# Un-normed products for the first four tiles behind a layer norm

## The chip, the cores and the metric

One NeuronCore of a Trainium2 chip runs the whole program. The metric is the device time of one execution in microseconds (us), of which less is better.

## The reference

The program computes two blocks of a transformer on 512 tokens (528 with the 16 meta tokens of the first block) of width 1024, in float32. The first block has two layers; each is a mixer and an MLP, and each of these four ends in a layer norm over the sum with the residual:

```python
h = _layernorm(DN_ALPHA * h + mix, ln_mix_g[l], ln_mix_b[l])
f = jnp.square(jax.nn.relu(h @ mlp_w1[l])) @ mlp_w2[l]
h = _layernorm(DN_ALPHA * h + f, ln_mlp_g[l], ln_mlp_b[l])
```

The mixer of layer 0 is a recurrence with attention, that of layer 1 a retention with the input projection `od_w_in`. The second block begins with `conv_w_in_2` and ends, in both of its layers, in a mixture of 64 experts. So behind each of the four norms of the first block stands a dense layer: norm 1 (`ln_mix` 0) feeds `mlp_w1` of layer 0, norm 2 (`ln_mlp` 0) feeds `od_w_in`, norm 3 (`ln_mix` 1) feeds `mlp_w1` of layer 1, and norm 4 (`ln_mlp` 1) feeds `conv_w_in_2`. A layer norm is (x - mean) * rs * g + b, where mean and rs = 1/sqrt(var + eps) belong to a token and g and b to a feature.

## The kernel before

Activations lie transposed: a feature tile of 128 features stands on the partitions and the tokens lie along the free dimension, so `hT` holds x as eight tiles of 128x528 (of 128x512 from the third norm on, where the meta tokens are dropped). The code numbers the norms l = 0 to 3; the text calls them first to fourth.

A dense layer is the generator `dense`. It makes output tiles of 128 columns. Float32 precision comes from splitting both operands into an upper and a lower part (`HS[:, 0]` and `HS[:, 1]` for the activations, `WS` for the weights) and adding three products: upper weights and lower weights times upper x, and upper weights times lower x. A tile with K = 1024 is eight k steps of three products; with 528 tokens each product is two matmuls of 264 columns, 48 in the tile, with 512 tokens one matmul of 512 columns, 24 in the tile. At a norm the first two tiles are made as a pair, k step by k step, the lower x products two steps behind, so that x may still be arriving (`pair`). `between` is a function called in front of step 4 of the pair, `late` one called in front of the last two k steps of the last tile.

Weights come by DMA from the SP queue into the five slots of `ring`, each with the weights of two tiles. ScalarE makes the upper part of a tile's weights (`split_hi`) and VectorE the lower one (`split_lo`), into one of three `WS` buffers, which is free when the tile three back is summed. Both stand in the program by hand, one for each tile, two tiles ahead of the product. Each engine executes its instructions in program order, so a split waits for all that is written ahead of it on its engine.

The sums lie in PSUM in four units of two banks that go round (`Ring`); `units.take` waits until the tile that held the unit has been read (`emptied`). `late` for a norm is `ln_first_pe`: for feature tiles 0 to 6 GpSimd has added up x (`S`) and x squared (`Q`) with `sums_pool`, and TensorE multiplies these with a vector of 1/1024 (one-column matmuls, which give the mean of each token on the partitions) and with a matrix of it (the mean of each token in a row on every partition).

Behind the last tile, `sum_dve` adds it to `hT[:, 7]`, ScalarE squares it (`square_act`), and `ln_pe` adds tile 7 to the statistics, in the units "stat" and "mean". VectorE (`ln_dve`) makes the variance, ScalarE the square root, VectorE the diagonal matrices `diag`, and TensorE spreads the root over all partitions (unit "rs"). Then eight feature tiles go through four engines: VectorE subtracts the mean row (`less`) and multiplies by g and the root (`scaled`), both with the row read from PSUM; ScalarE adds b twice, once into the upper half `HS[:, 0]` and once into `hT`; GpSimd subtracts the two into the lower half `HS[:, 1]` (`ln_pool`). The first matmul of the next layer waits for the upper half of feature tile 0.

In the MLP ScalarE applies ReLU to a w1 tile from PSUM into `tmpA`, GpSimd squares it, and ScalarE and VectorE split it into `BR`. The names in the profile are `sb_hs` for HS, `sb_ws` for WS, `sb_hT`, `sb_tmpA` (which holds S, Q, the squares and the ReLU rows), `sb_br`, `sb_VT` (g and b), `sb_cst` (the constants) and `ps` for PSUM. The text counts the tiles of the layer behind a norm from 0: the pair is tiles 0 and 1.

## Time and profile before

| | before |
|---|---|
| median of 3 runs | 3161.15 us (3158.59 to 3164.65) |
| profiled execution, first to last instruction | 3159.2 us |
| TensorE matmul busy | 2918.6 us, 92% |
| VectorE busy | 1399.3 us, 44% |
| ScalarE busy | 920.2 us, 29% |
| GpSimd busy | 608.3 us, 19% |
| share of TensorE in the chain that ended last | 86% |

The profiled execution has no time of its own in the results beside this span; what of an execution lies outside the first and last instruction is in the times of the runs alone. The four norms end near 290, 681, 1150 and 1518 us. Engines are PE (TensorE matmul), PEld (its weight loads), DVE (VectorE), ACT (ScalarE), POOL (GpSimd) and SP (its DMA queue). A line of the program is mostly that of a helper (L101 a matmul, L118 a tensor_tensor, L126 a scalar_tensor_tensor, L108 an activation, L112 a ScalarE copy), so groups are told apart by their tiles.

### The profile page before, as it was taken

How to read it: one execution, taken by the hardware profiler on the slowest of the kernel's cores; microseconds unless marked ns; L12 is line 12 of the kernel's file. 1: busy time of each engine (PE TensorE's matmuls, PEld its weight loads, DVE VectorE, ACT ScalarE, POOL GpSimd, SP SyncE). 2: the span in 40 equal slices, each digit the busy share in tenths (PEclk: the TensorE clock that was granted, in tenths of full speed). 3: DMA queues.
4: the chain of work that ended last, by engine and by line, in shares of the span. 5: the costliest groups of instructions: out<-in, count | busy, mean ns of one | idle time of the engine just before them, and what ended most of it. 6: DMA issues, size and time to landing. Idle time of an engine off the chain costs nothing.

```text
span 3159.2 us, 42475 instructions
## 1 busy us (share of the span) xinstructions
PE 2918.6 (92%) x17571; PEld 2268.3 (72%) x17571; DVE 1399.3 (44%) x2437; ACT 920.2 (29%) x1714; POOL 608.3 (19%) x534
## 2 busy tenths in 40 slices
PE   8999999999999999999999898888699997998884
PEld 7659999998888778888787555555577775555552
DVE  5634323343444543233544453323588844533234
ACT  4543313232222333142322121111335721211112
POOL 1404101120111131021100442222000002522220
PEclk9999999999999999999998899999899998999998
DMA  4012222222222222233225899999622139999996
GB/s 141 27 54 68 94 94 85 90 90 71 71 84 76 68 71 99 88 100 101 79 81 214 348 407 409 410 409 409 249 80 77 57 119 364 405 408 410 409 409 278
DMA packets 272213, 600.31 MB, mean 190 GB/s; under 512 B 32648, under 2 KB 177603, under 8 KB 255627
## 3 DMA queue, kind: packets, MB, share of 16 engines
q1 hardware_dynamic: 247552, 569.47, 47.9%
q0 software_dynamic: 23968, 27.93, 2.7%
q8 instruction: 143, 2.34, 0.3%
q14 instruction: 60, 0.48, 0.0%
q10 hardware_dynamic: 490, 0.08, 0.0%
HBM read 607.75 MB, written 39.89 MB: 205 GB/s over the span
## 4 chain that ended last, share of the span: by engine, by line
PE 86%; DVE 5%; issue 4%; ACT 2%; DMA 2%; POOL 1%; SPq 0%; ACTq 0%; DVEq 0%; POOLq 0%
PE ps L101 80%; PE ps L104 6%; DVE sb_tmpA L118 1%; DVE sb_arena L126 1%; DMA sb_arena<-in_exp_w_dram 1%; DVE sb_arena L118 1%; DVE sb_ws L118 1%; POOL sb_arena L118 0%; DMA sb_arena<-y_rows 0%; DVE sb_tmpA L129 0%; DMA sb_arena<-x_rows,sb_smallu 0%; ACT sb_arena L112 0%; ACT sb_hs L108 0%; ACT sb_hT L108 0%; DMA sb_arena<-in_x_dram 0%
## 5 line engine op out<-in xcount | busy, mean ns | idle before, releaser
L101 PE MATMUL ps<-sb_hs,sb_ws 128*128 128x264 f32 (+1 forms) x6384 | 1106.5, 335 | 17.2 <-ACT sb_hs L108 7.5
L101 PEld LDWEIGHTS ps<-sb_hs,sb_ws 128*128 128x128 f32 x6384 | 971.0, 190 | 148.2 <-issue 16.5
L118 DVE TENSOR_TENSOR sb_ws<-sb_ring,sb_ws 128x1024 fp32r<-128x1024 f32 x279 | 370.5, 1332 | 428.0 <-ACT sb_ws L112 427.5
L112 ACT CAST sb_ws<-sb_ring 128x1024 fp32r<-128x1024 f32 x279 | 290.8, 1046 | 333.6 <-PE ps L101 318.1
L101 PE MATMUL ps<-sb_arena 128*64 128x256 f32 (+18 forms) x1652 | 347.6, 420 | 26.6 <-issue 19.8
L101 PE MATMUL ps<-sb_br,sb_ws 128*128 128x264 f32 (+1 forms) x2304 | 367.4, 321 | 0.0
L101 PEld LDWEIGHTS ps<-sb_br,sb_ws 128*128 128x128 f32 x2304 | 332.4, 188 | 34.2 <-issue 0.5
L101 PE MATMUL ps<-sb_ring,sb_arena 128*64 128x256 f32 (+2 forms) x1506 | 284.0, 450 | 25.4 <-issue 22.6
L108 ACT ACTIVATE sb_arena<-ps 64x256 f32<-64x256 f32 (+6 forms) x188 | 73.8, 403 | 756.5 <-PE ps L101 733.8
L101 PEld LDWEIGHTS ps<-sb_arena 128*64 128x64 f32 (+6 forms) x1652 | 197.9, 160 | 128.7 <-issue 69.9
L104 PEld LDWEIGHTS ps<-sb_cst,sb_arena 128*128 128x128 f32 (+2 forms) x912 | 139.4, 209 | 170.6 <-DVE sb_arena L118 82.2
L118 DVE TENSOR_TENSOR sb_arena<-sb_arena,ps 64x256 f32<-64x256 f32 x128 | 54.3, 424 | 466.2 <-ACT sb_arena L108 466.1
L2705 POOL DMA_INDIRECT y_rows<-sb_arena,sb_smallu x128 | 132.7, 1037 | 642.4 <-PE ps L104 457.3
L101 PE MATMUL ps<-sb_hx,sb_arena 128*64 128x256 f32 (+1 forms) x1240 | 209.4, 449 | 26.2 <-issue 25.5
L104 PE MATMUL ps<-sb_cst,sb_arena 128*128 128x128 f32 (+2 forms) x912 | 178.1, 325 | 51.9 <-DVE sb_arena L123 20.5
L101 PEld LDWEIGHTS ps<-sb_ring,sb_arena 128*64 128x64 f32 (+1 forms) x1506 | 153.6, 145 | 94.2 <-issue 47.3
L112 ACT COPY sb_arena<-ps 128x128 f32<-128x128 f32 (+5 forms) x335 | 137.6, 449 | 279.2 <-PE ps L101 263.1
L101 PE MATMUL ps<-sb_wx,sb_arena 128*64 128x256 f32 (+1 forms) x880 | 181.2, 442 | 15.9 <-issue 15.8
L118 POOL TENSOR_TENSOR sb_tmpA<-sb_tmpA 128x528 f32<-128x528 f32 (+1 forms) x88 | 103.2, 1173 | 461.8 <-ACT sb_tmpA L108 461.8
L101 PEld LDWEIGHTS ps<-sb_hx,sb_arena 128*64 128x64 f32 x1240 | 118.0, 147 | 80.4 <-issue 46.0
L115 DVE COPY sb_arena<-ps 64x512 f32<-64x512 f32 (+3 forms) x155 | 107.6, 695 | 144.5 <-PE ps L101 123.1
L2701 POOL DMA_INDIRECT sb_arena<-x_rows,sb_smallu x128 | 133.1, 1040 | 96.7 <-DVE sb_smallu L126 45.1
(198 smaller groups left out, 2602.7 us busy)
## 6 DMA issues: line engine op xcount, KB each, us to landing
sb_ring<-in_exp_w_dram SPq DMA_DIRECT2D x113, 1024.0 KB
sb_hx<-in_exp_w_dram SPq DMA_DIRECT2D x92, 1024.0 KB
sb_arena<-in_exp_w_dram SPq DMA_DIRECT2D x66, 1024.0 KB
sb_wx<-in_exp_w_dram SPq DMA_DIRECT2D x66, 1024.0 KB
sb_ring<-in_mlp_w_dram SPq DMA_DIRECT2D x64, 1024.0 KB
sb_hT<-in_exp_w_dram SPq DMA_DIRECT2D x47, 1024.0 KB
sb_ring<-in_od_w_in_dram SPq DMA_DIRECT2D x24, 1024.0 KB
sb_ring<-in_conv_w_in_dram SPq DMA_DIRECT2D x12, 1024.0 KB
```

The source lines that it names most:

```text
L101: return self.e.matmul(o, l, r, start=start, stop=stop, skip_group_check=True)
L104: return self.e.transpose(o, i, ident)
L108: return self.e.activation(o, i, fn, bias=bias, scale=scale)
L112: return self.e.copy(o, i)
L115: return self.e.tensor_copy(o, i)
L118: return self.e.tensor_tensor(o, a, b, op)
L126: return self.e.scalar_tensor_tensor(out=o, in0=a, scalar=s, in1=b, op0=op0, op1=op1)
L2701: return e.e.indirect_dma_start(dst, None, Xh, bass.IndirectOffsetOnAxis(ap=ig[:, b:b + 1], axis=0), bounds_check=1023, oob_is_err=False)
L2705: return e.e.indirect_dma_start(Yh, bass.IndirectOffsetOnAxis(ap=isc[:, b:b + 1], axis=0), src, None, bounds_check=2047, oob_is_err=False)
```

## The change

The first four tiles (two column blocks) of the layer behind each norm take g*x, not yet normed, as their input: its upper and lower parts are made while the last product before the norm runs (`raw_act`, `raw_dve`), in free parts of the arena (`raw_of`). Since the norm of x is (x - mean) * rs * g + b, a product W(norm x) is rs * (W(gx) - mean * Wg) + Wb. Wg and Wb come out of the same product: two columns, g and b, stand behind the T tokens of each raw tile (`raw_vectors`), and `split_raw` makes the product in two halves, of T/2 and T/2 + 2 columns, in both banks of the unit, whatever T is.

The statistics of tile 7 (`ln_stats_pe`) and the root (`ln_root_pe`) are no longer made ahead of the layer but inside its pair, in front of k steps 2 and 5 (`between` becomes a table of steps). At the third norm `ln_first_pe` moves from behind the last tile into it. ScalarE copies the mean row and the root row out of PSUM (`mean_rows`), and `less` and `scaled` read the copies. The unit "stat" is gone at three norms: it lies in free columns of "mean".

The splits of the weights of tiles 2 and 3 move: one stands in front of the norm on ScalarE and behind `diag` on VectorE, one behind the last operation of the norm on both.

Each of the four raw tiles is normed behind its product: ScalarE copies Wg and Wb (`normed_vectors_act`), VectorE makes mean * Wg - product, then times rs (`normed_dve`), and ScalarE applies -1, Wb and the function (`normed_act`), which empties the unit. The other tiles of the layer take the normed x as before, and no longer start with a pair.

```diff
+        def raw_act(e, l, m):
+            T, (g, c) = span(l)[1], LNW[l]
+            ks = raw_group(l, m)
+            if m == 0 and l in half_read:
+                e.wait_ge(*summed["part", half_read[l]])
+            e.wait_ge(*dve_emptied[LNSTAGE[l], m])
+            if ks:
+                o, v = raw_vectors(l, 0, ks)
+                e.acp(o, v).then_inc(*x_hi.mark(("raw vectors", l, ks[0])))
+            e.act(raw_of(l, 0, m)[:, 0:T], of_norm(hT[:, m, :], l), ACT.Identity, scale=vec(g + "_g", 8 * c + m)).then_inc(
+                *x_hi.mark(("raw", l, m)))
+
+        def raw_dve(e, l, m):
...
+            e.stt(raw_of(l, 1, m)[:, 0:T], of_norm(hT[:, m, :], l), vec(g + "_g", 8 * c + m),
+                  raw_of(l, 0, m)[:, 0:T].bitcast(F), ALU.mult, ALU.subtract).then_inc(*x_lo.mark(("raw", l, m)))
...
+        def normed_dve(e, l, key, at, o, T):
+
+            first = span(l)[1] - T
+            mean, rs = (x[:, first:first + T] for x in mean_rows(l))
+            e.wait_ge(*act_ln["gb", key])
+            e.wait_ge(*summed[key])
+            e.wait_ge(*act_emptied["mean", l])
+            e.stt(halves(o), halves(mean), raw_vector_of(at)[0], halves(U_[key])[:, :, 0:T // 2], ALU.mult,
+                  ALU.subtract).then_inc(*dve_ln.mark(("less", key)))
+            e.wait_ge(*dve_ln["less", key])
+            e.wait_ge(*act_emptied["rs", l])
+            e.tt(o, o, rs, ALU.mult).then_inc(*dve_ln.mark(("z", key)))
+
+        def normed_act(e, key, at, o, fn, signal, mark):
+
+            e.wait_ge(*dve_ln["z", key])
+            e.act(o, o, fn, scale=-1.0, bias=raw_vector_of(at)[1]).then_inc(*signal.mark(mark))
...
+        def ln_hooks(e, units, l):
+
+            return {2: lambda: ln_stats_pe(e, l), 5: lambda: ln_root_pe(e, units.take(e, ("rs", l)), l)}
+
         def ln_act(e, l):
             g, i = LNW[l]
+            T = span(l)[1]
+            split_hi(e)
             e.wait_ge(*dve_ln["inv", l])
             n = len(span(l)[2])
             e.act(sm[:, 75:75 + n], sm[:, 70:70 + n], ACT.Sqrt).then_inc(*act_ln.mark(("rs", l)))
+            for x, what in zip(mean_rows(l), ("mean", "rs")):
+                e.wait_ge(*normed[what, l])
+                e.wait_ge(*dve_emptied["stat", l])
+                e.acp(fit(x, T), whole(U_[what, l], T)).then_inc(*act_emptied.mark((what, l)))
             for m in range(8):
...
+            split_hi(e)
...
+            split_lo(e)
+            mean, root = mean_rows(l)
 
             def less(m):
                 x = of_norm(hT[:, m, :], l)
-                e.wait_ge(*normed["mean", l])
-                e.tt(fit(x, T), fit(x, T), whole(U_["mean", l], T), ALU.subtract).then_inc(
-                    *dve_emptied.mark(("less", l, m), *([("mean", l)] if m == 7 else [])))
+                e.wait_ge(*act_emptied["mean", l])
+                e.tt(x, x, mean, ALU.subtract).then_inc(*dve_ln.mark(("less", l, m)))
...
-                e.stt(fit(x, T), fit(x, T), vec(g + "_g", 8 * c + m), whole(U_["rs", l], T), ALU.mult,
-                      ALU.mult).then_inc(*dve_emptied.mark(("scaled", l, m), *([("rs", l)] if m == 7 else [])))
+                e.wait_ge(*dve_ln["less", l, m])
+                e.wait_ge(*act_emptied["rs", l])
+                e.stt(x, x, vec(g + "_g", 8 * c + m), root, ALU.mult, ALU.mult).then_inc(*dve_ln.mark(("scaled", l, m)))
+            split_lo(e)
...
         def mlp_pe(e, units, l):
             for hf in range(2):
                 T = span(2 * l)[1]
-                dense_all(e, ("w1", l), [(2048 * hf + 256 * i, 256) for i in range(8)], 8, ln_x(2 * l), T, units)
+                cols = [(2048 * hf + 256 * i, 256) for i in range(8)]
+                if hf == 0:
+                    dense_all(e, ("w1", l), cols[:2], 8, raw_x(2 * l), T, units, True, ln_hooks(e, units, 2 * l), raw=True)
+                    cols = cols[2:]
+                dense_all(e, ("w1", l), cols, 8, ln_x(2 * l), T, units, hf > 0)
...
-            ln_pe(e, units, 2 * l + 1)
...
             for m in range(8):
                 split_hi(e)
                 square_act(e, ("out", 0), m, 0)
+                raw_act(e, 0, m)
             ln_act(e, 0)
```

VectorE at the end of the first norm, before: the last two `scaled` (the row with x2), then for each w1 tile a weight split (`sb_ws`) and a split of the squared ReLU (`sb_br`).

```order
L126 SCALAR_TENSOR_TENSOR sb_hT<-sb_hT,sb_VT,ps 128x528 x2
L118 TENSOR_TENSOR sb_ws<-sb_ring,sb_ws 128x1024
L118 TENSOR_TENSOR sb_br<-sb_tmpA,sb_br 128x528
L118 TENSOR_TENSOR sb_ws<-sb_ring,sb_ws 128x1024
L118 TENSOR_TENSOR sb_br<-sb_tmpA,sb_br 128x528
```

VectorE at the same place, with the change. The first split of weights is that of tile 3, the second that of tile 4.

```order
L126 SCALAR_TENSOR_TENSOR sb_hT<-sb_hT,sb_VT,sb_tmpA 128x528 x2
L118 TENSOR_TENSOR sb_ws<-sb_ring,sb_ws 128x1024
L126 SCALAR_TENSOR_TENSOR sb_tmpA<-sb_tmpA,sb_small,ps 128x528
L118 TENSOR_TENSOR sb_tmpA<-sb_tmpA 128x528
L126 SCALAR_TENSOR_TENSOR sb_tmpA<-sb_tmpA,sb_small,ps 128x528
L118 TENSOR_TENSOR sb_tmpA<-sb_tmpA 128x528
L118 TENSOR_TENSOR sb_br<-sb_tmpA,sb_br 128x528 x2
L118 TENSOR_TENSOR sb_ws<-sb_ring,sb_ws 128x1024
```

The second operand of `scaled` is now a row of `sb_tmpA`, no longer `ps`. In front of the splits of tiles 0 and 1 into `sb_br` stand two new operations for each tile, and the weight split of tile 4 stands behind all of them; before, the split behind the last `scaled` was that of tile 2.

ScalarE at the same place, as a piece of the difference: the last two rows of the norm, then the ReLU of the w1 tiles.

```order
 L108 ACTIVATE sb_hT<-sb_hT,sb_VT 128x528
 L112 CAST sb_ws<-sb_ring 128x1024
-L108 ACTIVATE sb_tmpA<-ps 128x528
-L112 CAST sb_br<-sb_tmpA 128x528
-L112 CAST sb_ws<-sb_ring 128x1024
-L108 ACTIVATE sb_tmpA<-ps 128x528
-L112 CAST sb_br<-sb_tmpA 128x528
-L112 CAST sb_ws<-sb_ring 128x1024
```

With the change the row of weights there is the upper part for tile 3, and what follows it is this:

```order
L112 COPY sb_small<-ps 128x2 x2
L108 ACTIVATE sb_tmpA<-sb_tmpA,sb_small 128x528
L112 CAST sb_br<-sb_tmpA 128x528
L108 ACTIVATE sb_tmpA<-sb_tmpA,sb_small 128x528
L112 CAST sb_br<-sb_tmpA 128x528
L112 CAST sb_ws<-sb_ring 128x1024
```

The ReLU of tile 0, which empties its unit, now reads what VectorE wrote in `sb_tmpA` and stands behind the copies of Wg and Wb; the upper weights of tile 4 stand behind both ReLUs.

## Rows read from the trace of the kernel before

**Rows 1.** Busy time of each engine, two stretches of 100 us among dense tiles (windows).

```profile
400.00:500.00 100.00, 100.00 (x820) 100.00 (x819) 27.78 (x27) 19.83 (x22) 2.66 (x2) 1.00 0.28 88
...
1300.00:1400.00 100.00, 100.00 (x434) 81.06 (x433) 31.28 (x33) 31.05 (x41) 13.57 (x12) 1.00 0.28 92
```

**Rows 2.** First norm in the timeline: start, us, engine, operation, xcount, [idle before <- releaser].

```profile
277.21 2.29 PE L101 MATMUL ps<-sb_cst,sb_tmpA 128*128 128x1 f32 x20
...
280.14 1.83 PE L101 MATMUL ps<-sb_hs,sb_ws 128*128 128x264 f32 x12
...
282.01 0.70 DVE L126 SCALAR_TENSOR_TENSOR sb_hT<-sb_hT,ps 128x528 f32<-128x528 f32 x1 [4.50 <-PE ps L101]
...
286.47 2.74 PE L101 MATMUL ps<-sb_tmpA,sb_cst 128*128 128x128 f32 x12
...
289.33 0.76 DVE L126 SCALAR_TENSOR_TENSOR sb_hT<-sb_hT,sb_VT,ps 128x528 f32<-128x528 f32 x1 [0.96 <-PE ps L101]
...
291.00 21.26 PE L101 MATMUL ps<-sb_hs,sb_ws 128*128 128x264 f32 x154 [1.79 <-ACT sb_hs L108]
...
291.70 11.11 POOL L118 TENSOR_TENSOR sb_hs<-sb_hT,sb_hs 128x528 fp32r<-128x528 f32 x8 [15.28 <-ACT sb_hT L108]
...
301.32 1.03 ACT L112 CAST sb_ws<-sb_ring 128x1024 fp32r<-128x1024 f32 x1
...
304.96 0.61 ACT L108 ACTIVATE sb_tmpA<-ps 128x528 f32<-128x528 f32 x1 [2.61 <-PE ps L101]
...
308.36 1.23 DVE L118 TENSOR_TENSOR sb_ws<-sb_ring,sb_ws 128x1024 fp32r<-128x1024 f32 x1 [0.24 <-ACT sb_ws L112]
...
316.96 0.61 ACT L108 ACTIVATE sb_tmpA<-ps 128x528 f32<-128x528 f32 x1 [1.02 <-PE ps L101]
```

**Rows 3.** Windows around the first norm; the PEclk column is the granted clock.

```profile
277.00:282.00 5.00, 4.97 (x40) 4.62 (x38) 0.50 (x1) 0.00 (x0) 0.00 (x0) 1.00 0.63 204
...
287.00:291.00 4.00, 2.21 (x12) 2.13 (x11) 3.04 (x6) 0.84 (x2) 0.00 (x0) 0.50 0.00 2
...
295.00:297.00 2.00, 2.00 (x15) 2.00 (x14) 2.00 (x4) 1.93 (x4) 1.93 (x2) 0.76 0.04 8
```

**Rows 4.** Timeline at norms 2 to 4: last sum, and reading of the fourth tile.

```profile
672.40 0.70 DVE L126 SCALAR_TENSOR_TENSOR sb_hT<-sb_hT,ps 128x528 f32<-128x528 f32 x1 [4.50 <-PE ps L101]
...
707.20 0.60 ACT L112 COPY sb_arena<-ps 128x528 f32<-128x528 f32 x1 [4.82 <-PE ps L101]
...
1138.62 0.69 DVE L126 SCALAR_TENSOR_TENSOR sb_hT<-sb_hT,ps 128x512 f32<-128x512 f32 x1 [1.16 <-PE ps L101]
...
1175.39 0.60 ACT L108 ACTIVATE sb_tmpA<-ps 128x512 f32<-128x512 f32 x1 [0.51 <-PE ps L101]
...
1511.64 0.69 DVE L126 SCALAR_TENSOR_TENSOR sb_hT<-sb_hT,ps 128x512 f32<-128x512 f32 x1 [3.81 <-PE ps L101]
...
1543.99 0.69 DVE L118 TENSOR_TENSOR sb_arena<-sb_tmpA,ps 128x512 f32<-128x512 f32 x1 [1.64 <-PE ps L101]
```

**Rows 5.** Groups by form, 280 to 1600 us: xcount | busy, mean ns | idle before.

```profile
L126 DVE SCALAR_TENSOR_TENSOR sb_hT<-sb_hT,sb_VT,ps 128x528 f32<-128x528 f32 x16 | 12.0, 757 | 2.1 <-PE ps L101 2.1
...
L118 DVE TENSOR_TENSOR sb_hT<-sb_hT,ps 128x528 f32<-128x528 f32 x16 | 11.0, 697 | 0.0
...
L118 POOL TENSOR_TENSOR sb_hs<-sb_hT,sb_hs 128x528 fp32r<-128x528 f32 x16 | 21.3, 1331 | 32.3 <-ACT sb_hT L108 31.4
```

**Rows 6.** Timeline of VectorE and of GpSimd, 794 to 812 us, both with SBUF operands.

```profile
794.84 4.70 DVE L118 TENSOR_TENSOR sb_tmpA<-sb_tmpA 128x512 f32<-128x512 f32 x4
...
799.46 4.55 DVE L118 TENSOR_TENSOR sb_ws<-sb_ring,sb_ws 128x1024 fp32r<-128x1024 f32 x2
...
795.62 7.31 POOL L118 TENSOR_TENSOR sb_arena<-sb_arena,sb_tmpA 128x512 f32<-128x512 f32 x4 [33.30 <-DVE sb_tmpA L118]
```

**Rows 7.** TensorE after 18.5 us without a matmul, and a window inside that time.

```profile
2256.16 1.97 PE L104 MATMUL ps<-sb_cst,sb_arena 128*128 128x128 f32 x8 [18.52 <-DVE sb_arena L123]
...
2242.00:2256.00 14.00, 0.00 (x0) 0.00 (x0) 8.65 (x9) 5.73 (x9) 0.00 (x0) 0.50 0.88 325
```

More of the change, by code:

```diff
@@ L318, in program @@
         named = {}
+        half_read = {}
         def piece(W, p0, nr, c0, n):
@@ L430, in split_lo, with dense @@
             e.tt(lo, part_view(p), hi.bitcast(F), ALU.subtract).then_inc(*w_lo.mark(p))
-        def dense(e, stage, cols, K, rhs, T, units, pair=True, between=None, order=by_columns, late=None):
+        def dense(e, stage, cols, K, rhs, T, units, pair=True, between=None, order=by_columns, late=None,
+                  raw=False):
+            between = between or {}
+            cut = split_raw if raw else split
             def next_part():
@@ L470, in dense @@
                     for k in range(kn + 2):
-                        if k == 4 and between is not None:
-                            between()
+                        if k in between:
+                            between[k]()
                         if k < kn:
@@ L663, in even_pe @@
             units.holder = [None] * 4
-            for m in dense(e, "win", CX[:4], 8, even_x, T1, main, True, lambda: tables_pe(e, side)):
+            for m in dense(e, "win", CX[:4], 8, even_x, T1, main, True, {4: lambda: tables_pe(e, side)}):
                 for c in GATES_AT.get(m, ()):
@@ L1196, in program, with raw_of @@
         LNSTAGE = [("out", 0), ("w2", 0, 1), ("out", 1), ("w2", 1, 1)]
[L1198 to L1201 removed]
+        def raw_of(l, half, k):
+            at = {0: (2112, 10560)[half] + 530 * k,
+                  2: (2112, 4762)[half] + 530 * k if k < 5 else (10560, 12150)[half] + 530 * (k - 5)}.get(
+                l, (0, 8448)[half] + 530 * k if k < 7 else (4240, 4770)[half])
+            return place_raw[:, at:at + 530]
@@ new lines, in raw_group @@
+        def raw_group(l, m):
+            late = RAW_LATE[l]
+            return tuple(k for k in range(8) if k not in late) if m == 0 else late if late and m == late[0] else ()
+        def raw_act(e, l, m):
[9 more added lines that the diff above has]
+                *x_hi.mark(("raw", l, m)))
@@ L1210, in ln_first_pe, with ln_stats_pe @@
                 for i, (o, a) in enumerate(stat[n * c:n * c + n]):
-                    e.mm(o, part[:, a:a + 128], onesn[:, 0:1], i == 0, False)
-            for o, a, b in split(units.take(e, ("mean", l)), T):
-                e.mm(o, onesn, s[:, a:b], True, False)
-        def ln_pe(e, units, l):
-            _, T, blocks = span(l)
-            x7, q7, diag = (of_norm(x, l) for x in (hT[:, 7, :], SQ1, SQ0))
-            n = len(blocks)
-            stat = stat_of(U_["stat", l], l)
+                    e.mm(o, part[:, a:a + 128], onesn[:, 0:1], i == 0 and (c == 0 or T == T1), False)
+            for o, a, b in split(u, T):
+                e.mm(o, onesn, s[:, a:b], T == T2, False)
+        def ln_stats_pe(e, l):
+            T, n = span(l)[1], len(span(l)[2])
+            x7, q7 = (of_norm(x, l) for x in (hT[:, 7, :], SQ1))
+            stat = stat_of(l)
             e.wait_ge(*dve_emptied[LNSTAGE[l], 7])
             for o, a in stat[0:n]:
-                t = e.mm(o, x7[:, a:a + 128], onesn[:, 0:1], False, True)
-            t.then_inc(*normed.mark(("first", l)))
+                e.mm(o, x7[:, a:a + 128], onesn[:, 0:1], False, True)
+            for o, a, b in split(U_["mean", l], T):
+                e.mm(o, onesn, x7[:, a:b], False, True)
             e.wait_ge(*act_ln["sq", l, 7])
@@ L1227, in ln_pe, with ln_root_pe @@
                 t = e.mm(o, q7[:, a:a + 128], onesn[:, 0:1], False, True)
-            t.then_inc(*normed.mark(("stat", l)))
-            for o, a, b in split(U_["mean", l], T):
-                t = e.mm(o, onesn, x7[:, a:b], False, True)
             t.then_inc(*normed.mark(("mean", l)))
-            uc = units.take(e, ("rs", l))
+        def ln_root_pe(e, uc, l):
+            _, T, blocks = span(l)
+            diag = of_norm(SQ0, l)
             for i, (t0, tn) in enumerate(blocks):
@@ L1258, in ln_dve @@
             st, diag = U_["stat", l], of_norm(SQ0, l)
-            e.wait_ge(*normed["first", l])
+            q = 512 if T == T1 else n
+            e.wait_ge(*normed["mean", l])
             e.cp(mu, st[:, 0:n]).then_inc(*dve_ln.mark())
@@ L1336, in mlp_act @@
                     out_splits(e, split_hi, m)
+                    if hf and m == 6:
+                        for k in range(6):
+                            raw_act(e, 2 * l + 1, k)
                     if hf:
                         square_act(e, ("w2", l, 1), m, 2 * l + 1)
+                    if hf and m >= 6:
+                        raw_act(e, 2 * l + 1, m)
             ln_act(e, 2 * l + 1)
```

167 lines of the change are left out of this document (125 added, 42 removed).

## The prediction

> **What bounds the kernel now.** I looked first at busy time by stretches of 100 us. Where dense tiles follow each other TensorE is 100% busy at full clock: 820 matmuls of 264 columns in 100 us, so 0.122 us each and 5.87 us for a tile of 48, and 434 of 512 columns, so 5.54 to 5.56 us for a tile of 24 [rows 1]. Only TensorE can be the bound there. The change touches the four places where that stream breaks, so I read the first of them in the timeline [rows 2]. VectorE starts to add out tile 7 at 282.01, which I take as zero. The first matmul of w1 starts at 291.00, the pair of tiles 0 and 1 is read at 304.96 (+22.9) and tile 3 at 316.96 (+34.9). Four tiles at 5.87 would have ended at +23.5: **each norm costs about 11 us**. In those 11 us the reader is to see a chain (statistics, a root, `less` and `scaled` on VectorE, bias on ScalarE) and a granted clock that falls to 0.50, after 1.00 shortly before [rows 3]. The other three look alike: from the last sum to the reading of the fourth tile 34.8, 36.8 and 32.35 us [rows 4]. So at most 4 x 11 us = 44 us could be had, and less, since the statistics and the root are TensorE work that stays.
>
> **The change, part by part (first norm; times from zero).**
>
> *Product first.* Tiles 0 and 1 need only g*x, split during the out tiles. TensorE no longer waits: 96 matmuls are 11.7 us. Inside the pair lie the statistics, the same 24 instructions as in the late block of tile 7, which runs from 277.21 to 280.14, 2.9 us [rows 2]; I take 3.0. The root is 12 instructions, 2.74 us at half clock [rows 2]; bounds 1.4 and 2.7, and I take 1.5, since the stream before it is dense. The pair ends at 11.7 + 3.0 + 1.5 = 16.2 and tile 2 at 22.1. Until here the change gains 6.7 us. The two added columns of a half (2 of 264) cost 0.04 us a tile; where T is 512 each matmul of 512 becomes two of 256 and 258, at 0.119 us each (between the two paces of rows 1) 5.7 instead of 5.55 us a tile. Both are nothing beside what follows.
>
> *Raw halves.* Eight more ScalarE and eight more VectorE operations per norm, 0.7 to 0.76 us each. In an out tile of 5.87 us VectorE has a weight split of 1.2 to 2.1, a sum of 0.70 and now 0.76: covered. In the w2 stages six come at once in front of sum 6: 6 x 0.7 us on VectorE, which moves that sum back by 0.7 to 1.0 us; its squares and their sums on GpSimd still end before the late block needs them. I cost this at nothing; if the cover went it would be about 1 us at two norms.
>
> *The chain of the norm.* Statistics end at 2.0 (two k steps) + 3.0 = 5.0. The small VectorE operations, the square root and the diagonals end at 7.4, but the root stands behind k steps 2 to 4 (36 x 0.122 = 4.4), so it starts at 9.4 and ends at 10.9; its copy out of PSUM (0.6) ends at 11.5. In the kernel before, the first `scaled` starts 7.3 after zero. **The norm starts 4 us later than before**: that is the price of standing inside the product.
>
> *less and scaled.* Sixteen VectorE operations, now with both tensors in SBUF where the second was in PSUM. Before they took 0.70 and 0.76 us and went at 1.3 us a pair while GpSimd subtracted beside them in 1.33 us each [rows 2, 5]; neither slowed the other. Rows with two SBUF operands look otherwise: four VectorE operations of 512 columns took 4.70 us together and the weight splits behind them 4.55 us for two, while four of GpSimd took 7.31, where one alone is near the 1.33 above [rows 6]. Laid on one line, 4 x 0.6 + 2 x 1.07 + 4 x 1.17 = 9.2 us is what lies between 794.84 and 804.01: they take turns and nothing overlaps (0.6, 1.07 and 1.17 are estimates of the work without its start-up, from the rows above: 0.70, 1.23 and 1.33 less 0.1 to 0.15). Here GpSimd's eight subtractions follow `scaled` two ScalarE operations behind; six of them fall between the first and the last `scaled`, and each holds VectorE for 1.33 less 0.2 = 1.14 us. So the eighth `scaled` ends at 11.5 + 0.8 + 7 x 1.2 (8.4) + 6 x 1.14 (6.8) = 27.5; without turns at 20.7.
> The Trainium skill says the same in "SBUF — State Buffer", section "SBUF: two separate sides": the port pair shared by VectorE and GpSimd is an exclusive lock, taken by a VectorE operation with two SBUF inputs, and the loser blocks. By that rule the `less` of before, with one input in PSUM, was free of it and the new one is not; the trace agrees for tensor_tensor (4.70 us for four) and shows no scalar_tensor_tensor with two SBUF inputs beside GpSimd.
>
> *Tile 3.* Its weight split stands behind all of this on both engines, and its PSUM unit is that of tile 0, which must be normed and read first. After the last `scaled`: the remaining bias operations at 1.39 us a pair (the pace of the eight subtractions, 11.11 us [rows 2]) until 29.7, ScalarE's half of the weights (1.03) 30.7, VectorE's (1.23, and 0.24 of waiting for its turn) 32.2, then for tile 0 mean*Wg - product 0.7, times the root 0.7, ReLU 0.6: 34.2. **TensorE stands from 22.1 to 34.2.** Tile 3 ends at 34.2 + 5.9 = 40.1 against 34.9. Tile 4's weight split comes after both tiles' norms and their br splits, at 41.0: 0.9 us more. Sum for the first norm +6.1 us. From tile 6 on the stream is whole again; nothing behind is slack that would give it back.
>
> *Clock.* A stand of 12 us lets the clock fall: with no matmul before 2256.16 for 18.5 us the granted clock of 2242 to 2256 is 0.50 [rows 7]. How long it stays down once a stream starts, the first norm shows: matmuls from 291.00 [rows 2], a clock of 0.76 in 295 to 297, so back at 296.0, 5 us at half rate [rows 3]. Bounds for one restart: 0 (if it stayed up) and 2.5 us (half of 5). I take 2.0, near the upper one, since the new stand is longer and complete, of which tile 4's 0.9 us of waiting hides part in the first norm: +1.1.
>
> *The other three.* Second norm (q tiles of 512, k tiles of 528): e0 at 33.9, fourth tile at 39.8 against 34.8, +5.0 and +2.0 of clock, +7.0. Third (T 512, its first statistics moved from behind tile 7 into it, the rest as above): +6.4 and about 0.5 of clock, +6.9; its splits keep waiting into tile 6. Fourth: unit of tile 0 free at 32.5, fourth tile at 38.2 against 32.35, +5.9 and +2.0, +7.9.
> Sum: 7.2 + 7.0 + 6.9 + 7.9 = **+29 us**. The profile's span, on which these times rest, is 3159.2; the runs shown are 3158.6 to 3164.7 with a median of 3161.15, which lies 2 us above it. Forecast 3161 + 29 = **3190 us**. With the unknowns that I named (clock 0 to 2.5 each: -7 to +4; root 0 to 1.2 each: +5) its own range is 3182 to 3200.
>
> **Rivals.** (1) *No turns.* The new `less` and `scaled` keep 1.3 us a pair beside GpSimd. For: the old ones did. Against: rows 6. Then the eighth `scaled` ends at 20.7, tile 0's unit is free at 27.8, TensorE stands 5.7 us a norm, tile 3 ends at 33.7 against 34.9 and, with the clock, each norm is -1 to +2.5: about +4 in all, 3165. If only the tensor_tensor half takes turns it is between, near 3177.
> (2) *It does what it says (the other side).* If tile 3 could start at 22.1, it would end at 28.0 against 34.9, -6.9 us a norm, and four norms give -27: 3134. It decides at one point: the unit and the weights of tile 3 would have to be there at 22.1. What stands in the queue behind the last `scaled` is 6.7 us, so the sixteen operations that start at 11.5 would have to end at 15.4, in 4 us; at 0.6 us each they need 9.2 with nothing in the way. I see only a wrong reading of the queues as a way there. For it speaks that the pair itself does end 6.7 us earlier. Half of the gain, through a shorter chain, is near -10: 3151.
> (3) *The clock falls inside the pair.* Statistics are one-column matmuls, and after 1.9 us of full work they last 3 us. Against: the same block at 277 to 280 kept 1.00 [rows 3]. If it falls, k steps 2 to 4 take 8.8 instead of 4.4 us, root and all behind it come 4.4 us later, four times: 3190 + 18 = 3208.
>
> **Numbers.** Forecast as computed 0.70 (3182 to 3200); turns for one half only 0.06; no turns 0.07; the gain, whole or in part, 0.07; clock inside the pair 0.10. 0.2% of the time is 6 us, which is about what separates a change from none here. Faster: 0.07 and a little of no turns, 0.08. Same: most of no turns, 0.07. Slower: 0.85. The range that leaves out 2 in 10 reaches to the half case below and the clock case above: 3171 to 3208.
>
> **What would show it.** TensorE's waits: a stand near 12 us in front of tile 3 at each of the four norms, released by ScalarE's ReLU or copy of tile 0 (`sb_tmpA` at norms 1, 3 and 4, `sb_arena` at 2). The pair ends at about +16, tile 2 at +22. VectorE's `less` or `scaled` near 1.8 us in turn with 0.7, GpSimd's `sb_hs` subtractions above 1.4. A clock of 0.50 around each stand. The prediction is wrong if `less` and `scaled` stay at 0.70 and 0.76, if tile 3 starts before +28, or if the clock is 0.50 in the pair.

## The result, and the profile after

The changed kernel takes **3192.28 us** (median of 4 runs, 3191.08 to 3195.41), the kernel before in the same job 3160.02 us (4 runs): ratio **1.0099, 95% interval 1.0085 to 1.0113**. The forecast was 3190. The profiled span is 3190.4 us against 3159.2, +31.2.

The first norm in the timeline of the changed kernel (columns as in [rows 2]):

```profile
283.22 2.14 PE L101 MATMUL ps<-sb_raw,sb_ws 128*128 128x264 f32 x16
...
292.73 1.41 PE L101 MATMUL ps<-sb_tmpA,sb_cst 128*128 128x128 f32 x12
293.99 11.61 PE L101 MATMUL ps<-sb_raw,sb_ws 128*128 128x264 f32 x92
317.69 8.86 PE L101 MATMUL ps<-sb_raw,sb_ws 128*128 128x264 f32 x48 [12.09 <-ACT sb_tmpA L108]
326.38 7.85 PE L101 MATMUL ps<-sb_hs,sb_ws 128*128 128x264 f32 x63
```

Tile 3 is the group of 48 at 317.69. In front of it TensorE is idle for 12.09 us (the text calls that a stand), where the kernel before had its stands in front of the first matmul [rows 2]. The rows of the other engines in that time:

```profile
283.42 0.70 DVE L126 SCALAR_TENSOR_TENSOR sb_hT<-sb_hT,ps 128x528 f32<-128x528 f32 x1 [4.67 <-PE ps L101]
...
294.89 0.77 DVE L126 SCALAR_TENSOR_TENSOR sb_hT<-sb_hT,sb_VT,sb_tmpA 128x528 f32<-128x528 f32 x1 [1.83 <-ACT sb_tmpA L112]
...
296.87 0.70 DVE L118 TENSOR_TENSOR sb_hT<-sb_hT,sb_tmpA 128x528 f32<-128x528 f32 x1
297.49 1.83 DVE L126 SCALAR_TENSOR_TENSOR sb_hT<-sb_hT,sb_VT,sb_tmpA 128x528 f32<-128x528 f32 x1
299.25 1.83 DVE L118 TENSOR_TENSOR sb_hT<-sb_hT,sb_tmpA 128x528 f32<-128x528 f32 x1
...
308.14 2.51 DVE L126 SCALAR_TENSOR_TENSOR sb_hT<-sb_hT,sb_VT,sb_tmpA 128x528 f32<-128x528 f32 x2
...
297.27 3.24 POOL L118 TENSOR_TENSOR sb_hs<-sb_hT,sb_hs 128x528 fp32r<-128x528 f32 x2 [20.28 <-ACT sb_hT L108]
...
316.81 0.73 ACT L108 ACTIVATE sb_tmpA<-sb_tmpA,sb_small 128x528 f32<-128x528 f32 x1 [2.86 <-DVE sb_tmpA L118]
```

From 297.27, when GpSimd begins to subtract, six of VectorE's operations take 1.80 to 1.83 us where the ones before took 0.70 and 0.77 (the x2 row at 308.14 is one of 1.83 and one of 0.76). The eighth `scaled` ends at 310.65, ScalarE reads tile 0 at 316.81, and tile 3 starts. The groups by form that answer to [rows 5]:

```profile
L126 DVE SCALAR_TENSOR_TENSOR sb_hT<-sb_hT,sb_VT,sb_tmpA 128x528 f32<-128x528 f32 x16 | 20.6, 1294 | 3.6 <-ACT sb_tmpA L112 3.6
...
L118 DVE TENSOR_TENSOR sb_hT<-sb_hT,sb_tmpA 128x528 f32<-128x528 f32 x16 | 15.5, 980 | 0.0
...
L118 POOL TENSOR_TENSOR sb_hs<-sb_hT,sb_hs 128x528 fp32r<-128x528 f32 x16 | 23.3, 1467 | 49.7 <-ACT sb_hT L108 49.5
```

TensorE's waits, all four norms (waited for: us in total, times, longest):

```profile
PE ps L101 <- ACT sb_tmpA L108: 36.2, 3, 12.1
...
PE ps L101 <- ACT sb_arena L108: 13.1, 3, 12.2
```

Four stands, of 12.09, 12.19, 12.06 and 12.10 us. The windows at the first, and two in tile 3 of the second, with the granted clock (PEclk) third from the right:

```profile
277.00:282.00 5.00, 5.00 (x32) 4.59 (x30) 1.75 (x2) 0.00 (x0) 0.00 (x0) 0.74 0.53 167
308.00:312.00 4.00, 0.00 (x0) 0.00 (x0) 2.65 (x3) 2.00 (x4) 1.72 (x2) 0.77 0.00 0
312.00:322.00 10.00, 4.31 (x19) 4.34 (x20) 4.96 (x6) 4.33 (x9) 4.74 (x4) 0.50 0.33 107
322.00:324.00 2.00, 2.00 (x11) 2.00 (x11) 1.50 (x2) 1.23 (x3) 0.00 (x0) 0.55 0.00 0
...
716.10:719.70 3.60, 3.60 (x16) 3.60 (x17) 1.87 (x3) 1.71 (x3) 0.00 (x0) 0.50 0.99 345
719.80:724.00 4.20, 4.20 (x36) 4.20 (x36) 2.33 (x3) 1.78 (x3) 0.00 (x0) 1.00 0.02 5
```

The clock is at its lower level, 1.2 GHz, when tile 3 starts and for 6.1, 3.7, 3.4 and 5.2 us of it at the four norms: tile 3 takes 8.86, 7.78, 7.49 and 8.28 us, where e4_fill below, in which the clock does not fall there, has 5.93 to 6.16. The first window shows a thing not foreseen: 0.74 in the late block of out tile 7, where [rows 3] had 1.00.

### The profile page after: what moved, and what is told of

The parts are those of the page before. It is cut to its first block, busy times and chain, and to the rows that moved or that the text cites. A ratio compares the mean times of both kernels' runs of the same rounds, so it can differ in the third digit from the quotient of the medians.

```text
span 3190.4 us, 43099 instructions
## 1 busy us (share of the span) xinstructions
PE 2907.6 (91%) x17811; PEld 2268.1 (71%) x17811; DVE 1460.0 (46%) x2506; ACT 951.9 (30%) x1781; POOL 614.4 (19%) x534
## 4 chain that ended last, share of the span: by engine, by line
PE 81%; DVE 7%; issue 4%; DMA 3%; ACT 2%; SPq 2%; POOL 1%; ACTq 0%; DVEq 0%; POOLq 0%
PE ps L101 76%; PE ps L104 5%; SPq L144 2%; DVE sb_tmpA L118 1%; DVE sb_hT L126 1%; DVE sb_hT L118 1%; DVE sb_arena L126 1%; DMA sb_hx<-in_exp_w_dram 1%; DMA sb_ring<-in_exp_w_dram 1%; DVE sb_arena L118 1%; DVE sb_ws L118 1%; DMA sb_arena<-y_rows 0%; POOL sb_arena L118 0%; DVE sb_tmpA L126 0%; DMA sb_arena<-x_rows,sb_smallu 0%
## 5 line engine op out<-in xcount | busy, mean ns | idle before, releaser
L101 PE MATMUL ps<-sb_hs,sb_ws 128*128 128x264 f32 (+1 forms) x5856 | 1008.0, 334 | 9.5 <-DVE sb_ws L118 4.6
L101 PEld LDWEIGHTS ps<-sb_hs,sb_ws 128*128 128x128 f32 x5856 | 885.5, 189 | 127.2 <-issue 8.3
L118 DVE TENSOR_TENSOR sb_ws<-sb_ring,sb_ws 128x1024 fp32r<-128x1024 f32 x279 | 363.0, 1305 | 433.6 <-ACT sb_ws L112 433.2
L104 PE MATMUL ps<-sb_cst,sb_arena 128*128 128x128 f32 (+2 forms) x912 | 175.7, 321 | 54.1 <-DVE sb_arena L123 22.2
L112 ACT COPY sb_arena<-ps 128x128 f32<-128x128 f32 (+4 forms) x335 | 137.6, 449 | 277.9 <-PE ps L101 264.4
## 6 DMA issues: line engine op xcount, KB each, us to landing
sb_arena<-in_exp_w_dram SPq DMA_DIRECT2D x66, 1024.0 KB, 21.6
```

The costliest lines, as they stand in the source:

```text
L101: return self.e.matmul(o, l, r, start=start, stop=stop, skip_group_check=True)
L104: return self.e.transpose(o, i, ident)
L112: return self.e.copy(o, i)
L118: return self.e.tensor_tensor(o, a, b, op)
```

## The experiments

Twelve kernels, each timed beside the kernel before on the same chip; differences to the changed kernel, and those of the last three kernels to e8_turns_back, are between medians of two jobs, and from job to job the median of the kernel before moved by up to 2.2 us. The first four take the changed kernel apart.

**e1_sub_late.** One line ahead of GpSimd's eight subtractions:

```diff
+            e.wait_ge(*dve_ln["scaled", l, 7])
             for m in range(8):
                 e.wait_ge(*act_ln["y", l, m])
```

> The changed kernel, but GpSimd's eight subtractions of a norm (sb_hs) wait until VectorE's eighth scaled is done; nothing else differs. My theory (turns): VectorE's less and scaled with two operands in SBUF take turns with GpSimd's subtractions. Then none of the sixteen is held any more: their means fall from 0.98 and 1.29 us to 0.70 and 0.76 us in all four norms, the eighth scaled ends about 6.8 us earlier, and the stand of TensorE in front of raw tile 3 falls from 12.1 to about 6 us. Most of that is given back behind it: GpSimd now begins its 8 x 1.33 = 10.7 us later, and tile 4 and the squares of tiles 0 and 1 wait for it; worked out for the first norm, tile 9 ends 1.7 us earlier than in the changed kernel, so about -7 us in all, near 3185 (3178 to 3190). Rival (no turns, the operations are long for another reason, such as reading two operands of SBUF): the means stay at 0.98 and 1.29 us, the stand stays at 12 us, and the time is the same or longer, 3192 to 3200.

3177.66 us, ratio to before 1.0050 (1.0036 to 1.0064), 14.6 us under the changed kernel. The forms:

```profile
L126 DVE SCALAR_TENSOR_TENSOR sb_hT<-sb_hT,sb_VT,sb_tmpA 128x528 f32<-128x528 f32 x16 | 12.0, 760 | 3.6 <-ACT sb_tmpA L112 3.6
...
L118 DVE TENSOR_TENSOR sb_hT<-sb_hT,sb_tmpA 128x528 f32<-128x528 f32 x16 | 11.0, 700 | 0.0
```

With GpSimd away, both forms are back at 0.76 and 0.70 us, with the same operands in SBUF. The stands in front of tile 3 are 6.20, 6.32, 7.47 and 7.52 us. So VectorE's operations were long because GpSimd ran beside them, and the rival is out. The gain is twice what I had expected. The four stands are 20.9 us shorter; of that 3.1 comes back in front of tile 4 (2.22 us at the first norm and 0.85 at the third, none at the other two) and 2.5 in a longer tile 3. My hand count had more coming back.

**e2_rows_psum.** `less` reads the mean's unit and `scaled` the root's unit in PSUM; all `less` come first.

```diff
-                e.tt(x, x, mean, ALU.subtract).then_inc(*dve_ln.mark(("less", l, m)))
+                e.tt(fit(x, T), fit(x, T), whole(U_["mean", l], T), ALU.subtract).then_inc(
+                    *dve_emptied.mark(("less", l, m), *([("mean", l)] if m == 7 else [])))
```

> The changed kernel, but less and scaled read the mean and the root from PSUM again (the copies in SBUF stay, for tiles 0 to 3), and all eight less come before the first scaled, so that the mean's unit is free in time for tile 2. GpSimd's subtractions run beside scaled as in the changed kernel. My theory (turns are a matter of two SBUF operands): less near 0.70 and scaled near 0.76 us beside GpSimd, GpSimd's subtractions back near 1.33; the eighth scaled ends some 8 us earlier (turns 6.8, and less that starts before the root), the stand in front of tile 3 is then 5 to 7 us, set by the eight pairs of bias operations of ScalarE, and by hand the four norms cost 4.3 us less each than in the changed kernel: about -17, near 3175 (3168 to 3183), still slower than the kernel before by some 15. Rival (VectorE's operations are long beside GpSimd wherever their second operand lies): scaled stays above 1.2 us, and the time is within 5 us of 3192.

3177.85 us, 1.0057 (1.0043 to 1.0072). `scaled` 756 ns, `less` 697 ns, the subtractions 1321 ns: as in [rows 5]. The stands in front of tile 3 are 7.93, 8.12, 5.08 and 8.36 us. The time is 3 us above the centre of what I expected; the third norm has a wait of its own, the root, which there takes the mean's unit and now stands until the last `less` (its end is at 1161.53):

```profile
1161.64 2.05 PE L101 MATMUL ps<-sb_tmpA,sb_cst 128*128 128x128 f32 x8 [3.78 <-issue]
```

**e3_early_tile3.** The norming of tiles 0 and 1 and tile 3's weight split stand between m = 2 and m = 3 on both engines (W is a weight split, v the copy of a tile's two vectors, n its two VectorE steps, e its reading by ScalarE):

```diff
+        EARLY_ACT = {2: 'W v0 v1 e0 e1'}
+        EARLY_DVE = {2: 'W n0 n1'}
```

> The changed kernel, but the norming of tiles 0 and 1 and the weight split of tile 3 stand between the scaled and bias steps of m = 2 and m = 3 on VectorE and ScalarE, not behind m = 7. My theory (the order of the queues holds tile 3, and the work that stands in the queues is what has to be done before TensorE can go on, wherever it stands): tile 3 follows tile 2 without a stand (it starts near +22 from VectorE's sum of out tile 7, as the change wants), and the stand moves to tile 4, whose input is the norm itself: 10 to 13 us in front of or inside tile 4. By hand tile 9 of the first norm ends only 1.4 us earlier than in the changed kernel: about -6 in all, near 3187 (3180 to 3193). Rival (only the unit and the weights of tile 3 were late, and with them in time the change does what it says): no stand over 3 us at tile 4, -6.9 us a norm against the kernel before, near 3134.

3182.82 us, 1.0071 (1.0057 to 1.0084):

```profile
292.75 17.85 PE L101 MATMUL ps<-sb_raw,sb_ws 128*128 128x264 f32 x140
322.67 17.55 PE L101 MATMUL ps<-sb_hs,sb_ws 128*128 128x264 f32 x126 [12.07 <-DVE sb_ws L118]
```

The 140 matmuls are the rest of the pair, tile 2 and tile 3 without a stand; then TensorE stands 12.07 us for tile 4's weights (8.21, 11.86 and 8.13 at the other norms). So tile 3 could start at +22, as the change wants, and that alone gains 9.5 us of the 32. The rival, no stand over 3 us, is out.

**e4_fill.** 88 matmuls in each stand:

```diff
+            for n in range(88):
+                x = raw_of(l, 0, n % 4)
+                e.mm(U_["rs", l][:, 0:264], x[:, 0:128], x[:, 0:264], True, True)
```

> The changed kernel with 88 matmuls of 264 columns added at each norm where TensorE stands in front of raw tile 3 (88 x 0.122 = 10.7 of the 12.1 us); they multiply two halves of g*x and write into the root's unit of PSUM after its copy; nothing reads the result. My theory (clock): TensorE's granted clock stays at 1.0 over the stand, and raw tile 3 takes 5.7 to 5.9 us at all four norms and not 8.86, 7.78, 7.49 and 8.28 as in the changed kernel; that is 9 us less in all, of which up to 1 is hidden at the first norm: -8, near 3184 (3181 to 3188). Rival (tile 3 is long for another reason than the clock, or the clock falls in any case because its load was high before): tile 3 stays above 7 us, and the time is 3190 to 3195.

3184.81 us, 1.0078 (1.0065 to 1.0091), 7.5 us under the changed kernel:

```profile
303.98 11.02 PE L101 MATMUL ps<-sb_raw 128*128 128x264 f32 x88
316.30 6.15 PE L101 MATMUL ps<-sb_raw,sb_ws 128*128 128x264 f32 x48 [1.30 <-ACT sb_tmpA L108]
...
312.00:322.00 10.00, 8.70 (x71) 8.52 (x70) 5.87 (x8) 4.18 (x9) 3.46 (x3) 1.00 0.34 105
```

The clock stays at 1.00 (last row, a window), and tile 3 takes 6.15, 6.16, 5.98 and 5.93 us: 8.2 us less over the four norms. New stands in front of tile 4 (0.66 us at the first norm, 0.72 at the third) take 1.4 of it back; the time shows 7.5. The clock's price is shown.

**e5_whole** takes all of it away at once. The main edits, beside the grouped `less` and `scaled` of e2:

```diff
+        EARLY_ACT = {1: 'W', 5: 'v0 v1 e0 W', 7: 'e1'}
+        EARLY_DVE = {7: 'W n0 n1 W'}
...
+                    units.holder[units.holder.index(("mean", l))] = ("rs", l)
+                    U_["rs", l] = U_["mean", l]
+                    e.wait_ge(*act_emptied["mean", l])
```

> The product of g*x for the first four tiles as in the changed kernel, with all that the four runs before named taken away at once: less all come before scaled, scaled reads the root from PSUM (no turns); the root is written into the mean's unit once the mean is copied, so that raw tile 3 takes that unit and not tile 0's; tile 3's weights are split behind m = 1 (ScalarE) and behind the eighth scaled (VectorE); tile 0 is normed and read, and tile 4's weights are split, behind m = 5; tile 1 is read behind m = 7; the splits of tiles 5 and 6 stand ahead of what waits for GpSimd's squares. My theory (what the change lost came from turns and from the order of work in the queues alone): TensorE goes from tile 2 to tile 3 and to tile 4 with stands under 2 us, the clock stays up, and by hand the fourth tile of the first norm ends at +28 (before +34.9, changed kernel +44.4) and tile 9 ends 6.1 us earlier than in the kernel before. Four norms: -24 against the kernel before, near 3138 (3132 to 3150). Rival (the bias steps of ScalarE, 8 x 1.39 us, and GpSimd's subtractions are still the chain, and the other two norms, which I worked out less closely, have stands of their own): 2 to 3 us a norm, 3150 to 3156. Third (nothing of the early start survives, since all 16 + 16 + 8 steps are still to be done before tile 4 ends): 3160 or more.

**3149.67 us, 0.9959 (0.9948 to 0.9971)**: faster than the kernel before, at the border between the first theory's range and the first rival. At the norms the first theory holds; behind the second and the fourth there are new stands:

```profile
291.65 17.54 PE L101 MATMUL ps<-sb_raw,sb_ws 128*128 128x264 f32 x140
309.59 35.61 PE L101 MATMUL ps<-sb_hs,sb_ws 128*128 128x264 f32 x289 [0.40 <-DVE sb_ws L118]
...
717.94 29.88 PE L101 MATMUL ps<-sb_hs,sb_ws 128*128 128x264 f32 x144 [4.79 <-DVE sb_ws L118]
...
1543.21 97.06 PE L101 MATMUL ps<-sb_hs,sb_ws 128*128 128x512 f32 x411 [4.06 <-DVE sb_ws L118]
```

**e6_own_unit** is e5_whole with `units.take(e, ("rs", l))` in place of the three lines on the mean's unit.

> As e5_whole, but the root has a unit of PSUM of its own again at norms 1, 2 and 4 (at the third it had one that stands in nobody's way, and that stays), so that raw tile 3 needs tile 0's unit. My theory (the unit is the second thing that tile 3 waits for, behind its weights): a stand of 4 to 5 us in front of tile 3 at the three norms until ScalarE's reading of tile 0 at about +26.6, and tile 9 of a norm ends 3.7 us later than in e5_whole: +11, near 3149 (3143 to 3156) if e5_whole is near 3138. Rival (the unit doesn't matter, the weights alone set tile 3): within 3 us of e5_whole.

3154.36 us, 0.9976 (0.9965 to 0.9987): +4.7, not +11. The stands in front of tile 3 are there (4.19, 4.39 and 4.70 us at norms 1, 2 and 4), so the unit does hold it; but the two stands of e5_whole further on are gone: the stream came later to them. A stand only costs what no other one behind it would have cost.

**e7_order** moves the weight splits that those two stands wait for, and the vectors of tiles 0 and 1:

```diff
-        EARLY_ACT = {1: 'W', 5: 'v0 v1 e0 W', 7: 'e1'}
+        EARLY_ACT = {1: 'W', 4: 'v0 v1', 5: 'e0 W', 7: 'e1'}
...
+                    e.cp(halves(vT[:, 0, :]), whole(U_["od", 16], T1)).then_inc(*dve_emptied.mark(("od", 16)))
+                    split_lo(e)
+                    split_lo(e)
                 e.wait_ge(*rot_in["all"])
...
-                if n == 2 or n >= 4:
+                if 2 <= n < 23:
```

> As e5_whole, with three stands removed that its trace shows behind the norms. (a) ScalarE copies the two vectors of tiles 0 and 1 behind m = 4 and not m = 5, so that VectorE norms them earlier and ScalarE no longer waits 1.9 us for tile 0; tile 4 stood 0.40, 0.59, 1.03 and 1.15 us for its weights. (b) At the second norm VectorE's splits of tiles 7 and 8 and the copy of tile 4 stand ahead of the rotation of q and k and not behind it; tile 7 stood 4.79 us for its weights. (c) At the fourth norm each weight split stands one tile earlier; tile 6 stood 4.06 us. My theory (these stands are all order in the queues): all three go, -12 against e5_whole, near 3138 (3134 to 3143). Rival (the engines beside TensorE are so full there that the stand only moves a tile on, as it did from tile 3 to tile 4 before): 2 to 6 us less than e5_whole, 3144 to 3148.

**3135.84 us, 0.9918 (0.9905 to 0.9932)**, 26 us faster than before and 56 faster than the changed kernel. At the four norms TensorE has no stand left; the first:

```profile
292.28 17.54 PE L101 MATMUL ps<-sb_raw,sb_ws 128*128 128x264 f32 x140
309.66 35.62 PE L101 MATMUL ps<-sb_hs,sb_ws 128*128 128x264 f32 x290
...
285.00:335.00 50.00, 50.00 (x409) 49.90 (x409) 35.71 (x49) 29.03 (x46) 20.29 (x15) 1.00 0.20 64
```

**e8_turns_back** puts `scaled` back on SBUF in that order:

```diff
-                e.stt(fit(x, T), fit(x, T), vec(g + "_g", 8 * c + m), whole(U_["rs", l], T), ALU.mult,
+                e.stt(x, x, vec(g + "_g", 8 * c + m), root, ALU.mult, ALU.mult).then_inc(
```

> As e7_order, but scaled reads the root from its copy in SBUF and so takes turns with GpSimd's subtractions again (less are all done before GpSimd begins and are free of it either way); the root's unit is free as soon as it is copied. My theory (turns hold the norm wherever the queue order lets GpSimd run beside scaled): scaled at 1.2 us or more and not 0.74 to 0.76, the eighth ends some 4.5 us later, and about 3 us a norm reach TensorE's stream in front of tiles 3 and 4: +8 to +12 against e7_order, near 3148. Rival (in the better order the turns are hidden, since ScalarE's bias steps at 1.39 us each set the pace and scaled at 1.2 us stays ahead of them): within 3 us of e7_order.

3140.53 us, 0.9933 (0.9919 to 0.9947): +4.7. Neither text has it right, for `scaled` is not held at all; GpSimd is:

```profile
294.70 5.52 DVE L126 SCALAR_TENSOR_TENSOR sb_hT<-sb_hT,sb_VT,sb_tmpA 128x528 f32<-128x528 f32 x8
300.13 1.22 DVE L118 TENSOR_TENSOR sb_ws<-sb_ring,sb_ws 128x1024 fp32r<-128x1024 f32 x1
...
297.08 17.41 POOL L118 TENSOR_TENSOR sb_hs<-sb_hT,sb_hs 128x528 fp32r<-128x528 f32 x8 [20.47 <-ACT sb_hT L108]
```

Eight `scaled` in 5.52 us, 0.69 each. GpSimd's eight by themselves (duration in ns min/median/max, first and last start):

```profile
L118 POOL TENSOR_TENSOR sb_hs<-sb_hT,sb_hs x8: 1333/1810/5462, 297.1 to 312.2; 128x528 fp32r<-128x528 f32 x8
```

Its first subtraction took 5.46 us, until 302.54. Less the 1.33 that one takes alone, it waited from 297.08 to 301.2, through the rest of one `scaled`, four more, and the weight split behind them, which is a tensor_tensor and was not held either. So my theory of the turns, that a VectorE operation with two SBUF operands waits for GpSimd, was too simple. The last four kernels ask which of the two waits.

**e9_less_first** is the changed kernel with the order alone changed:

```diff
-            less(0)
+            for m in range(8):
+                less(m)
             for m in range(8):
                 x = of_norm(hT[:, m, :], l)
-                if m < 7:
-                    less(m + 1)
```

> The changed kernel with one edit: VectorE does the eight less in one run and then the eight scaled in one run, not by turns (less of m + 1, scaled of m). All of them still read two operands in SBUF. It follows from the trace of e8_turns_back, where eight such scaled in one run took 0.69 us each beside GpSimd's subtractions, while the first of these had to wait over 4 us. New theory (who gets the port depends on how VectorE's operations follow each other: in a run of the same operation it keeps it, by turns it lets GpSimd in): scaled at 0.75 and less at 0.70 us, GpSimd's subtractions above 1.8 us in the mean, the stand in front of tile 3 at 7 to 9 us and not 12.1, and the time like that of e2_rows_psum, 3178 (3172 to 3184). Rival (the old one: any VectorE operation with two SBUF operands takes turns with GpSimd; in e8_turns_back something else kept GpSimd away): scaled at 1.3 us or more, stand 11 us or more, 3187 to 3194.

3178.79 us, 1.0058 (1.0045 to 1.0072), 13.5 us under the changed kernel from the order alone. The stands in front of tile 3 are 9.10 to 9.43 us, just above the 7 to 9 that I expected. Neither `less` nor `scaled` is held, and GpSimd pays:

```profile
L126 DVE SCALAR_TENSOR_TENSOR sb_hT<-sb_hT,sb_VT,sb_tmpA 128x528 f32<-128x528 f32 x16 | 11.0, 760 | 0.0
...
L118 POOL TENSOR_TENSOR sb_hs<-sb_hT,sb_hs 128x528 fp32r<-128x528 f32 x16 | 28.3, 1811 | 42.7 <-ACT sb_hT L108 42.7
```

**e10_by_turns** is the reverse edit on e8_turns_back.

> e8_turns_back with one edit: less of m + 1 and scaled of m by turns, as in the changed kernel. New theory: VectorE is held again, five or six of its sixteen operations a norm for 1.1 us each, means near 1.0 and 1.2 us, the eighth scaled ends some 6 us later, and TensorE stands 2 to 4 us a norm in front of tile 3 or 4: +8 to +15 against e8_turns_back, 3149 to 3156. Rival (in the better order of the queues GpSimd never meets these operations, and it doesn't matter how they follow): means at 0.70 and 0.76 us, within 3 us of e8_turns_back.

3166.60 us, 1.0022 (1.0013 to 1.0031): +26 from the order alone, more than the 15 I had as the upper end. `scaled` has 1157 ns, `less` 983 ns, GpSimd 1522 ns, and TensorE stands 6.27 us in front of tile 3 at the first norm.

**e11_with_gaps** makes each `scaled` of e8_turns_back wait until the one before has written.

> e8_turns_back with one edit: each scaled waits until the scaled before it has written (the eight still stand in one run), so that there is a gap of some 0.1 us between them. If VectorE keeps the port only because its next operation is ready before the last one ends, GpSimd gets in at the gaps: scaled near 1.3 us or more, GpSimd's subtractions back under 1.6 us. If what counts is that the operations are of one kind, nothing changes but the gap: scaled starts every 0.8 us, not held, and GpSimd's mean stays above 2 us.

3162.61 us, 1.0010 (1.0001 to 1.0019), +22. The gap of 0.1 us is enough to let GpSimd in (`scaled` 1345 ns in the mean, the subtractions 1526):

```profile
297.04 11.49 DVE L126 SCALAR_TENSOR_TENSOR sb_hT<-sb_hT,sb_VT,sb_tmpA 128x528 f32<-128x528 f32 x8
...
303.17 6.52 POOL L118 TENSOR_TENSOR sb_hs<-sb_hT,sb_hs 128x528 fp32r<-128x528 f32 x4 [0.66 <-ACT sb_hT L108]
```

**e12_far_turns**: four `less`, then `scaled` of m and `less` of m + 4 by turns, then four `scaled`.

> e8_turns_back with one edit: four less come first, then scaled of m and less of m + 4 by turns, then the last four scaled in a run. So the operations still go by turns from about 292 to 298 us at the first norm, where GpSimd's first subtraction comes at about 295, but scaled reads what less wrote eight operations earlier and not two. If what lets GpSimd in is that scaled needs a result written just before (a gap too short to see in the starts), nothing is held: means at 0.70 and 0.76 us and the time of e8_turns_back, within 3 us. If it is the change from one kind of operation to the other, the scaled and less between 295 and 298 are held, two or three of them a norm at 1.8 us, and the eighth scaled ends 2 to 3 us later than in e8_turns_back: +3 to +8.

3159.37 us, 0.9996 (0.9986 to 1.0005), +19, where I had 3 at most for the one theory and 3 to 8 for the other. Held in spite of the far operand, so it is not the result written just before. But it isn't the change of kind alone either, which the weight split in e8_turns_back spoke against too:

```profile
295.35 1.84 DVE L126 SCALAR_TENSOR_TENSOR sb_hT<-sb_hT,sb_VT,sb_tmpA 128x528 f32<-128x528 f32 x1
297.11 1.84 DVE L118 TENSOR_TENSOR sb_hT<-sb_hT,sb_tmpA 128x528 f32<-128x528 f32 x1
298.87 6.66 DVE L126 SCALAR_TENSOR_TENSOR sb_hT<-sb_hT,sb_VT,sb_tmpA 128x528 f32<-128x528 f32 x5
```

The last five are of one kind, and at 1.33 us in the mean (median 1.80) three of them are held. In e8_turns_back and e9_less_first GpSimd came for the first time within a run of eight and was kept out; here it had been let in before the run began. What decides is left open. TensorE stands 4.36 to 4.76 us at each norm in front of tile 3, which is most of the 19.

## Why the prediction was right

The path was the one forecast, and the time came so near partly by luck: the clock cost 2.6 us more than the sum had, and the other terms 1.8 us less.

*Pair, tile 2, root.* From zero (283.42) the root starts at +9.3, its copy ends at +11.35 and tile 2 at +22.2; the prediction has 9.4, 11.5 and 22.1.

*Turns.* The eighth `scaled` ends at +27.2 (27.5), six operations are held for 1.05 to 1.13 us. It was argued from tensor_tensor rows alone [rows 6], and the prediction says that the trace before has no scalar_tensor_tensor with two SBUF inputs beside GpSimd. It has one, in the recurrence, the last of three, which took 1.72 us where the other two took 0.77:

```profile
52.16 3.33 DVE L126 SCALAR_TENSOR_TENSOR sb_arena<-sb_arena,sb_VT 128x528 f32<-128x528 f32 x3
53.49 1.43 POOL L118 TENSOR_TENSOR sb_arena<-sb_arena 128x528 f32<-128x528 f32 x1 [6.30 <-ACT sb_arena L108]
```

The trace after shows it for `scaled`, and e1_sub_late that nothing else made the operations long. Rival 1 is out. For this order the term was right; as a rule it was not: e9_less_first has the same operands beside the same subtractions and nothing held, 13.5 us less. The step "they take turns and nothing overlaps" holds in that one of the two waits, but not in which of them, nor for how long: GpSimd waited through six operations of VectorE.
The Trainium skill, "SBUF — State Buffer", section "SBUF: two separate sides", calls the port an exclusive lock whose loser blocks. The traces agree that one of the two waits: in one order VectorE loses (1.83 us), in the other GpSimd does (5.46 us for its first subtraction in e8_turns_back, of which 4.1 are waiting).

*The stand.* Predicted 12.1, measured 12.06 to 12.19. Tile 4's weights are there in time at the first norm, since tile 3 took so long: the 0.9 is hidden.

*Clock.* Taken as 2.0 a restart, less what was hidden; against e4_fill tile 3 was longer by 2.7, 1.6, 1.5 and 2.4 us, 8.2 in all where the sum had 5.6. The bound of 2.5 was too low at the first norm: I had read the time at half rate as 5 us, and it was 6.1 there, but 3.7 and 3.4 at the second and third. The range's "-7" for the clock is a slip: the sum has only 5.6 to take away.

*Sum by norm.* The start of the last sum lies 1.41, 9.62, 19.44 and 23.54 us later than before at the four norms [rows 2, 4], and the end 31.2. The third norm's first statistics (1153.82 to 1156.07, 2.25 us) now stand ahead of that sum. So the norms cost 8.2, 7.6, 6.35 and 7.7 us, 29.8 together, where the prediction had 7.2, 7.0, 6.9 and 7.9. Without the clock that is 21.6 against 23.4. Most of the difference lies at the third norm, 4.9 for 6.4: there the prediction had weight splits that keep TensorE waiting into tile 6, and the trace has one wait of 0.26 us in front of it. The first 1.41 us are the dip of the clock in the late block, which I had not foreseen: I had only [rows 3], where the same block kept 1.00. It is chance (last section), and no part of the forecast.

*Rival 2* was said to decide at one point, tile 3's unit and weights at +22.1. e3_early_tile3 gave them in time and the stand moved to tile 4, so that point was named too narrowly: what has to be in time is the norm itself on VectorE, ScalarE and GpSimd. And I held "a wrong reading of the queues" to be the only way to 3134; e7_order gets to 3136 with the same product first, by the order of the queues, the root in the mean's unit, and `scaled` reading PSUM (the last worth 4.7 us by e8_turns_back). *Rival 3* is out: the k steps inside the pair ran 36 matmuls in 4.52 to 4.66 us, at full clock, at all four norms.

## What to carry to other kernels

A product moved ahead of its norm only pays if the engines that norm keep pace with it: list what stands in each queue between the new start and the first tile that needs the normed input, and move weight splits and the reading of the first tiles in between, or the stand only moves on a tile. Where VectorE and GpSimd both work in SBUF, put VectorE's operations in one run without waits before GpSimd starts, or give them an operand in PSUM; the order alone was worth 13 us in one kernel and 26 in another, though by what rule is open. Price each stand of TensorE that lets the clock fall at its own length plus up to 2.8 us.
